# Eight products of the identity with itself between the small products of the samples' own states

## What is computed

```python
def step(S, inp):                      # wkv7_scan, from S0 = state_wkv for the samples
    r_t, w_t, k_t, v_t, kk_t, a_t = inp
    sa = jnp.einsum('bhij,bhj->bhi', S, kk_t)
    S = (S * w_t[:, :, None, :]
         - sa[..., None] * (kk_t * a_t)[:, :, None, :]
         + v_t[..., None] * k_t[:, :, None, :])
    y = jnp.einsum('bhij,bhj->bhi', S, r_t)
    return S, y
```

## Time and profile before

| what | value |
|---|---|
| median of three timed runs | 1561.86 us (1559.67 to 1563.74) |
| the profiled execution | 1562.55 us |
| its span on the core | 1560.8 us |
| TensorE (PE) busy | 1519.3 us, 97% |
| VectorE (DVE) busy | 964.9 us, 62% |
| ScalarE (ACT) busy | 663.3 us, 42% |
| GpSimd (POOL) busy | 122.3 us, 8% |
| mean granted clock of TensorE | 0.99 |

### The profile page before, as it was taken

One profiled execution on the slowest core, in us unless ns is written; L12 is line 12 of the kernel. 1 busy time (PEld: TensorE's weight loads), 2 busy tenths in 40 slices (PEclk: granted clock), 3 DMA queues, 4 the chain that ended last, 5 costly groups with the idle time before them and its releaser, 6 DMA issues.

```text
span 1560.8 us, 34167 instructions
## 1 busy us (share of the span) xinstructions
PE 1519.3 (97%) x14080; PEld 1421.3 (91%) x14080; DVE 964.9 (62%) x1392; ACT 663.3 (42%) x1029; POOL 122.3 (8%) x183
## 2 busy tenths in 40 slices
PE   8999999999999999999999999999988889999998
PEld 8999998988888799999999999999954449999998
DVE  6655446686897476555457655644688876655532
ACT  5443334663664654343344334333344445434331
POOL 0000000002231200000000333000001210000000
PEclk9999999999998999999999999999999999999999
DMA  8766673440010466756774554444889995444442
GB/s 270 237 215 204 221 222 110 136 135 16 17 30 10 121 205 213 232 192 216 230 239 162 184 164 147 152 149 149 331 307 408 408 382 163 138 159 144 146 149 81
DMA packets 241004, 288.54 MB, mean 185 GB/s; under 512 B 18898, under 2 KB 221922, under 8 KB 240754
## 3 DMA queue, kind: packets, MB, share of 16 engines
q1 hardware_dynamic: 237234, 281.20, 53.3%
q0 software_dynamic: 3648, 5.57, 1.4%
HBM read 280.39 MB, written 39.90 MB: 205 GB/s over the span
## 4 chain that ended last, share of the span: by engine, by line
PE 89%; DVE 6%; ACT 2%; issue 1%; DMA 1%; POOL 0%; SPq 0%; DVEq 0%; ACTq 0%
PE ps L762 25%; PE ps L763 25%; PE ps L764 24%; PE ps L1068 4%; PE ps L1063 3%; DVE ring L2867 1%; PE ps L816 1%; PE ps L1519 1%; DMA ring<-in_cache_v 1%; PE ps L1203 1%; PE ps L1219 1%; PE ps L1158 1%; PE ps L1094 1%; ACT ring L1893 0%; DMA arena<-in_x_sample 0%
## 5 line engine op out<-in xcount | busy, mean ns | idle before, releaser
L762 PE MATMUL ps<-arena_r,ring_r 128*128 128x320 f32 (+1 forms) x2024 | 626.8, 310 | 1.7 <-DVE arena L2530 1.7
L764 PE MATMUL ps<-arena_r,ring_r 128*128 128x320 f32 (+1 forms) x2024 | 624.4, 309 | 0.0
L2261 DVE TENSOR_TENSOR ring_r<-ring,ring_r 128x2048 fp32r<-128x2048 f32 (+2 forms) x131 | 291.5, 2227 | 252.0 <-ACT ring_r L1714 146.1
L762 PEld LDWEIGHTS ps<-arena_r,ring_r 128*128 128x128 f32 x2024 | 380.7, 188 | 5.6 <-issue 4.8
L764 PEld LDWEIGHTS ps<-arena_r,ring_r 128*128 128x128 f32 x2024 | 380.8, 188 | 0.0
L763 PE MATMUL ps<-arena_r,ring_r 128*128 128x320 f32 x1136 | 351.8, 310 | 0.0
L763 PE MATMUL ps<-xn_r,ring_r 128*128 128x320 f32 (+2 forms) x888 | 272.7, 307 | 0.0
L763 PEld LDWEIGHTS ps<-arena_r,ring_r 128*128 128x128 f32 x1136 | 213.9, 188 | 0.2
L2261 DVE TENSOR_TENSOR arena_r<-arena,arena_r (+3 forms) x155 | 141.6, 924 | 109.8 <-ACT arena_r L1714 48.9
L762 PE MATMUL ps<-arena_r 128*128 128x320 f32 x592 | 183.2, 309 | 0.0
L764 PE MATMUL ps<-arena_r 128*128 128x320 f32 x592 | 182.9, 309 | 0.0
(11 more groups left out here) (386 smaller groups left out, 1828.4 us busy)
## 6 DMA issues: line engine op xcount, KB each, us to landing
ring<-in_ffn_w_in SPq DMA_DIRECT2D x66, 1024.0 KB, 5.1
k_grouped<-in_cache_k SPq DMA_DIRECT2D x64, 512.0 KB, 5.4
ring<-in_ffn_w_out SPq DMA_DIRECT2D x24, 1024.0 KB, 5.1
arena<-in_cache_v SPq DMA_DIRECT2D x45, 512.0 KB, 9.9
ring<-k_grouped SPq DMA_DIRECT2D x44, 512.0 KB, 7.8
arena<-in_ffn_w_in SPq DMA_DIRECT2D x21, 1024.0 KB, 5.1
ring<-in_rw_w_rkv SPq DMA_DIRECT2D x11, 1024.0 KB, 5.0
arena<-k_grouped SPq DMA_DIRECT2D x20, 512.0 KB, 8.2
```

The costliest lines, as they stand in the source:

```text
L762: pe.matmul(out, part(s, 1)[:, k, cs], x_hi, start=first_, stop=False)
L764: return pe.matmul(out, part(s, 0)[:, k, cs], x_hi, start=False, stop=last)
L2261: return TT(out, x, high.bitcast(F32), ALU.subtract)
```

## The change

`own_state` gets one product more for each `q`: the identity by the identity, 128 rows by 128 columns, into bank `t`, columns `q * 128` to `q * 128 + 127`. These are the columns that the four products of head 0 of the same `q` write: together they write each column of this part of bank `t` again, with `start=True`, so nothing of the added product is left in the result. With four `q` in each of two calls there are eight added products, sixteen matmul instructions and sixteen weight loads. No semaphore wait is added, and no other engine's program is changed.

```diff
@@ -1151,6 +1151,7 @@
                 dve_done(first[f"state_in{CHUNKS - 2}"] + 1)
                 for q in range(4):
                     p = 4 * hf + q
+                    mm = mmul(ps[:, t % 8, q * P:(q + 1) * P], ident, ident)
                     for g in range(2):
                         for j in range(2):
                             cc, to = p * T + TP + (4 * g + j) * QS, q * P + g * C + j * QS
```

## The result

The changed kernel is slower: median 1566.93 us (1562.51 to 1570.16, 20 runs) against 1560.55 us (1557.79 to 1564.79, 20 runs), ratio 1.004 with an interval of 1.0032 to 1.0047. That is 6.4 us, more than the 4.7 us that I had set as the bound of "no change", and above my range of 1558.6 to 1565.4.

A forecast was written before the change was run, and what follows sets the result against it. TensorE was taken to bound the kernel. Products cost +1.8 us; losing the first low-clock stretch saves 3.0, the second 1.3; with one of them going, the middle is -0.4 from 1561.86, hence 1561.5 us, range 1558.6 to 1565.4.

The forecast's parts named there:

- What bounds the kernel: TensorE, busy 97% of the span and 89% of the chain, with both `own_state` calls on it.
- Part 1: Eight added identity products in `own_state` cost 1.8 us at full clock, all on the chain, with no wait added.
- sign of being wrong: The prediction fails if, among other things, an added product in `own_state` costs over 0.3 us at full clock.
- the rival on weight loads: In `own_state`, sixteen identity weight loads at 188 ns stay unhidden, adding 3.0 us: 1564.5 us, chance 0.04.
- Parts 2 and 3: Half-clock stretches from the first and second `own_state` calls cost 3.0 and 1.3 us; ACT limits the second saving.
- one of the two stretches goes: One low-clock stretch at the `own_state` calls vanishes, or each in part: middle -0.4 us, 1561.5 us, chance 0.41.
- rival C: Low-clock stretches at `own_state` last half as long again, 3.0 us more in all: 1567.2 us, chance 0.07.
- ACT as the next bound: Behind the second `own_state` call, if the clock holds, ACT copies `X4` without waiting for TensorE, 5.0 us later.
- Rival A: Both low-clock stretches at the `own_state` calls go, -2.5 us: 1559.4 us, chance 0.25.
- Rival B: Neither low-clock stretch at the `own_state` calls goes; the products only add work, +2.3 us: 1564.2 us, chance 0.23.
- rival D: Sixteen identity weight loads in `own_state` that nothing hides, 3.0 us on top of the forecast: 1564.5 us, chance 0.04.
- within 0.3%: Whole kernel's time lands within 4.7 us of no change, 1557.2 to 1566.5 us, chance 0.91.

The follow-up runs named there:

- e2: Changed kernel with each call's four identity products in one block ahead of its 32 thin products; ratio to the kernel before 1.0014.
- e3_elsewhere: Kernel before, with the eight identity products put among small products in chunk 3 and `own_state` untouched; ratio to before 1.0035.
- e4: Changed kernel with each identity product replaced by a single-instruction fp32r product of the centring matrix with itself; ratio to the kernel before 1.0037.
- e7: Kernel before, with the thin products of the first `own_state` call done twice and no identity products; ratio to before 1.0056.
- e9: Changed kernel with each identity product cut into two of 64 rows, for the banks of heads 0 and 1; ratio to the kernel before 1.0002.
- e11_wide128: Kernel before, no product added, the j = 0 thin products widened to 128 moving columns (64 at each bank's last); ratio to before 0.9986.
- r1_before: The kernel before, unchanged, profiled and timed once more; ratio to its earlier runs 1.0006.

## Why the prediction was wrong

The forecast was 0.4 us below before, and the means differ by 6.2 us the other way. Of these 6.6 us, 2.0 are the price of the products (3.8 at equal clock, not 1.8), and 4.6 are the clock: the forecast took the middle of 3.0 and 1.3 us as saved, 2.2, and 2.4 us were lost. So two steps failed, and the one on the clock weighs more.

**What bounds the kernel: right.** TensorE carries the chain, the added time arrived, and no wait was added.

**Part 1, the price of the products: the first step that failed.** I took 1.8 us from line 956 and called 3.7 the upper end. Measured: 4.4 us in a place with undisturbed clock, 3.8 at equal clock in the change, 0.5 us each, which is over the 0.3 us that the prediction named as its sign of being wrong. The work was sized right (0.22 us for a product that follows another); the missing term is the switch between operands of 64 and of 128 rows and back, 0.3 us for each of eight places, 2.4 us. Both rows I leaned on were streams of one form, and so was the dense stream of the earlier trace rows, which I used to dismiss the rival on weight loads. The Trainium skill, "TensorE: Matmul & The Clock Gate", section "The mechanism" (the prediction named the section after it), says that a weight load overlaps products in flight only when the row groups differ. The traces agree at a switch, where a place costs 0.3 us more, and not in a stream of one form, where full-row instructions follow each other at 0.11 us in the block of e2 and at 0.15 us in the dense stream, though the record of a load lasts 188 ns. I had given this rival a chance of 0.04 and 1564.5 us; its price alone, 3.0 us for sixteen loads, was close to the 2.4 us that the switches took.

**Parts 2 and 3, what the low stretches cost: the sizes right, the reading not.** 3.0 + 1.3 = 4.3 us for 13.6 us of low clock, against 45.2 - 40.4 = 4.8 us by the local measure, or 0.35 us for each us of low clock; the line over all runs, 0.69 for each us lost, says the same, since a us at 0.50 counts as half a us lost. That a low stretch behind the second call is cheap shows in e3_elsewhere, where 3.4 us of it cost 0.2. But I took the one profile for the typical execution; its repetition had a quarter of that low clock. What there was to gain was smaller than my sum said.

**The forecast itself, "one of the two stretches goes": the second step that failed, and the larger one.** I weighed the 1.8 us of full-width work as a dose that could help the clock or do nothing, and apart from rival C gave no term to the case that the change makes it worse. Measured: more clock was lost than before, 17.4 us a run against 13.9, and the same products in a block lost 14.8. The runs thus show that spreading them costs clock; that it does so because TensorE stays longer in thin work, with little added work, is argued from e2, e4, e7 and e9 and not shown. What the prediction read from the rows, that thin work loses clock without waiting, was right: e7 repeats it.

**ACT as the next bound: right.** In e11_wide128, where the clock holds, ACT (start, us, instruction, idle before) copies `X4` without having waited for TensorE, 5.2 us behind the call's end at 504.27:

```profile
504.37 1.56 ACT L1977 ACTIVATE ring<-ps 64x256 f32<-64x256 f32 x4 [3.29 <-PE ps L1171]
505.96 1.55 ACT L1903 ACTIVATE ring<-ps 64x256 f32<-64x256 f32 x4
507.53 1.91 ACT L1724 ACTIVATE ring_r<-ring 128x2048 fp32r<-128x2048 f32 x1
509.46 0.66 ACT L1892 ACTIVATE xn<-ps 128x256 f32<-128x256 f32 x2
```

TensorE then stood idle for 1.24 us and went on at 509.95, behind the first of the two copies at 509.46 (the trace names no releaser for this wait):

```profile
509.95 1.15 PE L1068 MATMUL ps<-xn,extra 64*64 64x64 f32 x32 [1.24 <-issue]
```

**Forecast and rivals.** "One of the two goes" looked right in the profile of the changed kernel (10.2 us low instead of 13.6) and was wrong over the runs: the lost clock rose by 3.5 us. Rival A (both go) is seen only in the profiles with four products a place, with half-row products, or with wider thin ones. Rival B (neither goes) was nearest in kind, and 2.7 us short of the measured median. Rival C (the clock is down longer) was the right direction, for a reason I had not named: I thought of the added products running at half clock, and the runs point to the longer stay in sparse work ahead of the fall. No low stretch of the last chunk in the two profiles of the change is longer than 6.83 us, so its mechanism did not happen in them. The measured excess is made up like rival C's term for the clock (3.0 us, measured 2.4) plus rival D's for the loads (3.0 us, measured 2.0 to 2.5), two cases that I had held for unlikely each and never together.

**The chances.** 0.91 for "within 0.3%" rested on a ceiling for the price that no row of an interleaved product supported, and on a clock that the change could leave alone or mend but hardly worsen.

## What to carry to other kernels

A filler that shall keep TensorE's clock should have the row form of its neighbours; here it otherwise paid 0.3 us at each place before it had done anything. Better still, as e11_wide128 did, widen the products that are there, where more moving columns cost no time, into columns that are overwritten later. Price an inserted instruction by a row in which two forms alternate, not by a stream of one form. And where the clock differs from execution to execution, read it from many runs (mean clock by run) and not from one profile.

## What the runs showed of the hardware

- Thin products (64 rows by 128 columns of weights, 32 moving columns) lose the clock without idle time ahead of the fall: in e7, in a row of them that lasted 10.6 us, it fell from 1.00 to 0.50 after 3.6 us, in all of which TensorE was busy. It does not fall every time: both calls of r1_before ran through at 1.00, the first one ending 0.2 us ahead of a fall.
- Moving columns behind a 128-column load are free from 32 up to a mean of 76 (half of the products at 128, except the last of each bank at 64): 3.69 us for a call either way (r1_before, e11_wide128).
- A change from 64-row to 128-row operands and back costs 0.3 us beyond the work at full clock, beside thin and beside dense neighbours alike (0.53 us in the changed kernel and 0.54 us in e3 for a product that costs 0.22 us behind another).
